# A first norm whose root is applied to the product's result too, its scales and weights loaded first; the roots of four feed-forward norms spread by a product on a repeated column

## What is computed

```
def rmsnorm(x, g):
    y = xf * lax.rsqrt(jnp.mean(xf * xf, axis=-1, keepdims=True) + RMS_EPS)
    return (y * g.astype(jnp.float32)).astype(x.dtype)
...
    for l in range(DEPTH):
        h = rmsnorm(x, norm_mix[l])
        (u_ssm, q_lat, kv_lat, k_rope, hg_q, hg_f, hg_i, hg_g, gate_logits) = jnp.split(h @ w_in[l], split_at, axis=-1)
        y_ssm = s5_mixer(u_ssm, ...)
...
        x = x + swiglu_ffn(rmsnorm(x, norm_ffn[l]), ffn_w_gate_up[l], ffn_w_down[l])
```

## Time and profile before

| | |
|---|---|
| median of 3 executions | 1955.02 us (1954.1 to 1955.06) |
| the profiled execution's own time | 1958.95 us |
| its span (first to last instruction) | 1957.1 us |
| TensorE busy | 1831.5 us, 94% |
| VectorE busy | 1163.9 us, 59% |
| ScalarE busy | 869.0 us, 44% |
| GpSimd busy | 164.0 us, 8% |
| mean DMA rate | 140 GB/s |

### The profile page before, as it was taken

How to read it: one execution, slowest core, us unless ns; L and a number is a source line. 1 busy time by engine, 2 the same in 40 slices (tenths; PEclk the granted TensorE clock), 3 DMA queues, 4 the chain that set the end, 5 groups by cost and what they waited for, 6 DMA issues and landing times.

```text
span 1957.1 us, 26609 instructions
## 1 busy us (share of the span) xinstructions
PE 1831.5 (94%) x9873; PEld 1417.2 (72%) x9873; DVE 1163.9 (59%) x1871; ACT 869.0 (44%) x1417; POOL 164.0 (8%) x203
## 2 busy tenths in 40 slices
PE   7999999989999999999888999998899999889998
PEld 6675556569898865556577998646799874669987
DVE  7993545545667893545454556565477746546775
ACT  4223434355345422334455445436455543555553
POOL 4000004020000000002112000101300000130000
PEclk9999999999999999999999999998999999899999
DMA  5444333335455444434153556431355544135553
GB/s 158 129 131 141 119 129 118 131 112 162 152 182 195 119 132 130 140 124 156 44 178 116 180 186 193 147 119 54 119 173 173 182 152 125 59 97 164 171 189 134
DMA packets 192357, 274.58 MB, mean 140 GB/s; under 512 B 25616, under 2 KB 129540, under 8 KB 192228
## 3 DMA queue, kind: packets, MB, share of 16 engines
q1 hardware_dynamic: 191364, 269.86, 44.2%
q0 software_dynamic: 864, 3.02, 0.5%
HBM read 271.78 MB, written 1.05 MB: 139 GB/s over the span
## 4 chain that ended last, share of the span: by engine, by line
PE 81%; DVE 8%; ACT 5%; issue 3%; POOL 1%; DMA 0%; SPq 0%; DVEq 0%; ACTq 0%; POOLq 0%
PE bank L390 41%; PE bank L388 30%; DVE WL L1132 2%; ACT WH L1375 2%; PE bank L649 1%; PE bank L570 1%; POOL WL L1132 1%; PE bank L992 1%; PE bank L578 1%; PE bank L842 1%; PE bank L473 1%; DVE bank L2022 1%; ACT HTH L1375 1%; PE bank L696 1%; DVE HTL L1969 1%
## 5 line engine op out<-in xcount | busy, mean ns | idle before, releaser
L1375 ACT ACTIVATE WH<-W 128x1024 fp32r<-128x1024 f32 x328 | 347.5, 1060 | 325.8 <-PE bank L390 251.8
L1132 DVE TENSOR_TENSOR WL<-W,WH 128x1024 fp32r<-128x1024 f32 x288 | 353.1, 1226 | 229.4 <-ACT WH L1375 221.1
L390 PE MATMUL bank<-HTH,WH 128*128 128x256 f32 x1536 | 440.9, 287 | 24.6 <-DVE WL L1132 14.7
L390 PE MATMUL bank<-HTL,WH 128*128 128x256 f32 x1536 | 436.5, 284 | 0.0
L390 PE MATMUL bank<-HTH,WL 128*128 128x256 f32 x1536 | 436.4, 284 | 0.0
L390 PEld LDWEIGHTS bank<-HTH,WH 128*128 128x128 f32 x1536 | 296.5, 193 | 31.3 <-DVE WL L1132 17.7
L390 PEld LDWEIGHTS bank<-HTL,WH 128*128 128x128 f32 x1536 | 296.8, 193 | 0.5 <-issue 0.5
L390 PEld LDWEIGHTS bank<-HTH,WL 128*128 128x128 f32 x1536 | 296.6, 193 | 0.0
L388 PE MATMUL bank<-W,HTF 128*128 128x512 f32 (+1 forms) x576 | 230.1, 557 | 0.0
L390 PE MATMUL bank<-WH,HTH 128*128 128x512 f32 x480 | 196.1, 409 | 15.5 <-POOL WL L1132 9.3
L390 PE MATMUL bank<-WH,HTL 128*128 128x512 f32 x480 | 191.8, 400 | 0.0
(11 more groups left out here) (400 smaller groups left out, 2208.0 us busy)
## 6 DMA issues: line engine op xcount, KB each, us to landing
W<-in_w_in SPq DMA_DIRECT2D x132, 512.0 KB, 3.6
W<-in_ffn_w_gate_up SPq DMA_DIRECT2D x176, 256.0 KB, 3.1
W<-in_w_up SPq DMA_DIRECT2D x176, 256.0 KB, 3.1
W<-in_ffn_w_down SPq DMA_DIRECT2D x44, 512.0 KB, 4.2
W<-in_w_down SPq DMA_DIRECT2D x44, 512.0 KB, 4.3
W<-in_w_out SPq DMA_DIRECT2D x32, 512.0 KB, 4.0
W<-in_ssm_w_glu SPq DMA_DIRECT2D x16, 512.0 KB, 3.6
W<-in_x_w_kv SPq DMA_DIRECT2D x16, 512.0 KB, 4.1
```

What stands on the lines that cost most here:

```text
L390: m = pe.matmul(out, at_a(a[x]), at_b(b[y]), start=(start and i == 0), stop=(stop and i == 2), skip_group_check=True)
L1132: eng.tensor_tensor(WL[:, m % HSLOTS, 0:width], W[:, n % RSLOTS, 0:width], h, ALU.subtract)\
L1375: copy = lambda dst, src, scale=1.0: act.activation(dst, src, ACT.Copy, scale=scale)
```

## The change

Four things change.

1. The first layer's first norm is treated like the second layer's: TensorE transposes `X` itself, the eviction multiplies by the scale alone (into `HTLF`), `ssm_u` runs on that, and VectorE multiplies each `u` by `RB` as it evicts it. VectorE also writes `HTF` = `HTLF` times `RB` for the products behind it (two instructions on 128x1024). VectorE's second half of `setup_states` becomes `setup_steps` and stands behind that, and the second group of phases stands between the `u`.
2. The 16 rows of `norm_mix` are loaded on their own, right behind `X`, then the first weight chunk, then the other parameters, then the other chunks. TensorE transposes the scales alone first (`par0`), and the other parameters between the first and the second `u`. GpSimd makes the identity and the index tables first, masks later.
3. `token_row` no longer needs the copy in `SCR`: the stationary operand is the column of `RSTD` itself, repeated 128 times by its access pattern. It waits for the root alone. GpSimd's copies are gone.
4. In the four feed-forward layers `token_row` stands behind the last chunk of pair 0, one chunk earlier.

```diff
             def token_row(n):
 
-                pe.wait_ge(sem["rstd_rows"], rows_at[n])
+                pe.wait_ge(sem["rstd"], n + 1)
                 ps = begin("rb", n)
                 for tt in range(TT):
-                    m = pe.matmul(ps[:, tt * P:tt * P + P], RSR[:, tt, :], IDENT[:, :], start=(tt == 0),
+                    m = pe.matmul(ps[:, tt * P:tt * P + P], RSTD[:, n, tt:tt + 1].broadcast_to([P, P]), IDENT[:, :], start=(tt == 0),
                                   stop=(tt == TT - 1), skip_group_check=True)
...
+                    pe.wait_ge(sem["x_rows"], 16)
+                    for j in range(4):
+                        raw_T(nrm, j, None)
...
-                    src = HTLF if l else HTF
+                    src = HTLF
...
-                ssm_u(0, 1)
                 if l:
-                    token_row(mix_norm)
+                    ssm_u(0, 1)
+                else:
+                    ssm_u(0)
+                    parameters()
+                    ssm_u(1)
+                token_row(mix_norm)
                 ssm_u(2)
...
-                if l:
-                    pe.wait_ge(sem["mix_scaled"], 1)
+                pe.wait_ge(sem["mix_scaled"], l + 1)
...
-                            if (j, k0) == (1, 0):
+                            if (j, k0) == (0, KT - 2):
                                 token_row(n)
...
+            sp.dma_start(R1[0:16, :], T["norm_mix"].rearrange("l (k p) -> (l k) p", p=P)).then_inc(sem["mix_rows"], 16)
...
             for n, (name, srcs, k, cols) in enumerate(chunks):
+                if n == 1:
+                    first_params()
...
-                if n in rows_at:
-                    signal(pool.tensor_copy(RSR, RSTD[:, n, :].rearrange("p (t o) -> p t o", o=1)
-                                            .broadcast_to([P, TT, P])), "rstd_rows", rows_at[n])
...
-                    norm_rows(nrm, X)
-                    norm_cols(nrm, "norm_mix", l)
+                    whole_cols(nrm, HTLF, mix_gain, 0)
+                    whole_cols(nrm, HTLF, mix_gain, 2)
+                    sum_x()
+                    parameters()
                     setup_states()
...
-                else:
-                    for q in range(4):
-                        take_u(q)
```

More of the change, by code:

```diff
@@ L465, in raw_T @@
             def raw_T(n, j, tag):
-                for tt in range(TT):
+                for tt in range(TT) if tag else ():
                     freed(*tag, tt, j // 2)
@@ L1542, in take_PT, with sum_x, parameters @@
                 evict(t_buf(tag, i).rearrange("p a b -> p (a b)"), tag, "t", m)
[L1544 to L1550, removed]
-            ps = bank(("par",))
-            copy(PAR[:, 0:NR1], ps[:, 0:NR1])
-            free_after(copy(PAR[:, C3:CLS + 32], ps[:, C3:CLS + 32]), "par")
-            signal(act.activation(SST[:, 0, :], PAR[:, CLS:CLS + 32], ACT.Exp), "sst_step", 1)
+            wait_full(act, ("par0",))
+            free_after(copy(PAR[:, 0:16], bank(("par0",))[:, 0:16]), "par0")
+            def sum_x():
+                act.wait_ge(sem["x_rows"], 16)
+                for tt in range(TT):
+                    ins = act.activation(XN[:, tt, :], X[:, tt, :], ACT.Square, scale=DM ** -0.5,
+                                         accum_out=SSQ[:, 0, tt:tt + 1])
+                    if tt < TT - 1:
+                        link(ins)
+                signal(ins, "ssq", 1)
+            def parameters():
+                act.wait_ge(sem["params"], 16 * N_PARAMS)
+                signal(copy(LSB.rearrange("p (g c) -> p g c", g=2), LSR.rearrange("p (g o) -> p g o", o=1)
+                            .broadcast_to([32, 2, 64])), "ls_rows", 1)
+                full("par")
+                ps = bank(("par",))
+                copy(PAR[:, 16:NR1], ps[:, 16:NR1])
+                free_after(copy(PAR[:, C3:CLS + 32], ps[:, C3:CLS + 32]), "par")
+                signal(act.activation(SST[:, 0, :], PAR[:, CLS:CLS + 32], ACT.Exp), "sst_step", 1)
             def tables(l, q):
@@ L2166, in setup_states, with setup_steps @@
                 signal(tt_(e[:, 1, :], lb1, d, ALU.subtract), "sst", 1)
-                for q in range(2):
-                    for _ in phases(0, q):
-                        pass
+            def setup_steps():
+                lre, lim = PAR[:, C3:C3 + 32], PAR[:, C3 + 32:C3 + 64]
                 dve.wait_ge(sem["sst_act"], 1)
@@ L2273, in _, with take_u @@
             for l in range(DEPTH):
+                def take_u(q):
+                    wait_full(dve, ("u", l, q))
+                    free_after(tt_(UT[:, q, :], bank(("u", l, q))[:, 0:S], RB, ALU.mult), "u", l, q)
+                mix_gain = lambda k: gain("norm_mix", l, k, KT)
                 if l == 0:
-                    norm_rows(nrm, X)
-                    norm_cols(nrm, "norm_mix", l)
+                    wait_freed(dve, ("par0",))
+                    for j in (1, 3):
+                        whole_cols(nrm, HTLF, mix_gain, j)
@@ L2277, in _ @@
                     setup_states()
                 else:
-                    def take_u(q):
-                        wait_full(dve, ("u", l, q))
-                        free_after(tt_(UT[:, q, :], bank(("u", l, q))[:, 0:S], RB, ALU.mult), "u", l, q)
-                    add_whole(nrm, HTLF, lambda k: gain("norm_mix", l, k, KT), ("ffd", l - 1), RSTD[:, nrm - 1, :])
-                    for _ in phases(l, 2):
-                        pass
-                    wait_freed(dve, ("rb", nrm))
-                    take_u(0)
@@ L2288, in _ @@
-                    take_u(1)
-                    for _ in phases(l, 3):
-                        pass
-                    take_u(2)
-                    for j in range(0, KT // 2, 2):
-                        wait_freed(dve, ("hT", nrm, j))
-                    for k in range(0, KT, 4):
-                        ins = tt_(HTF[:, k:k + 4, :], HTLF[:, k:k + 4, :],
-                                  RB.rearrange("p (o t) -> p o t", o=1).broadcast_to([P, 4, S]), ALU.mult)
-                    signal(ins, "mix_scaled", l)
@@ L2298, in _ @@
-                    take_u(3)
+                    add_whole(nrm, HTLF, mix_gain, ("ffd", l - 1), RSTD[:, nrm - 1, :])
+                for _ in phases(l, 2 if l else 0):
+                    pass
+                wait_freed(dve, ("rb", nrm))
+                take_u(0)
+                take_u(1)
+                for _ in phases(l, 3 if l else 1):
+                    pass
+                take_u(2)
+                for j in range(0, KT // 2, 2):
+                    wait_freed(dve, ("hT", nrm, j))
@@ L2299, in _ @@
+                for k in range(0, KT, 4):
+                    ins = tt_(HTF[:, k:k + 4, :], HTLF[:, k:k + 4, :],
+                              RB.rearrange("p (o t) -> p o t", o=1).broadcast_to([P, 4, S]), ALU.mult)
+                signal(ins, "mix_scaled", l + 1)
+                take_u(3)
+                if l == 0:
+                    setup_steps()
                 nrm += 1
```

83 lines of the change are left out of this document (44 added, 39 removed).

## The result

The changed kernel takes 1945.56 us (median of 6 executions, 1943.12 to 1946.9), the kernel before 1955.11 on the same chip (6 executions, 1954.1 to 1959.31). The ratio is 0.9943, 95% interval 0.993 to 0.9956: 11.2 us less, between 8.6 and 13.7, where 7.1 was forecast. The direction was right and the size too small. A second measurement gave 0.9941 (0.9922 to 0.9959).

What follows compares the result with a forecast made beforehand. TensorE, busy for 94% of the span, was taken as the bound. Feed-forward layers 5.8, second layer's norm 0 and start 1.3 summed to 7.1 us off 1955.02, so 1947.9 us, range 1945 to 1951.5.

Steps and rivals of the forecast that it cites:

- Feed-forward layers: TensorE's waits for `WL` at the four feed-forward starts go: 5.8 us gained, bounds 4.2 to 6.2.
- The repeated column: `token_row` with the repeated column costs the same as the load from `SCR`: 0 us, at worst 3 us lost.
- The second layer's norm: Second layer's first norm: the 0.4 us wait for GpSimd's copy ends, TensorE waits for VectorE's scaling instead; 0.0 us gained.
- The start: Kernel start, up to the long products: 1.3 us gained, taken between 2.2 and 0.5; range −1.0 to 3.2.
- Both ends of the bound: At the start, the range's ends: −1.0 if half speed lasts into the long products, 3.2 if SyncE's rows come sooner.
- SyncE's rows came 1.0 us sooner: At the start, rows were put at 29.8; a microsecond sooner, with three chunks in a row instead of four, gave 3.2.
- the pause costs more: Rival at the start: TensorE stays at half clock into `hf`, −1.0 instead of 1.3, 1950.2 us; start worth nothing or less: 0.18.
- VectorE at the start: VectorE's set-up begins at 14 and the first scan at 35.2, 2.5 us sooner, so VectorE takes nothing back.
- The stall did not move elsewhere: Rival in the four feed-forward layers: the stall moves, 0.9 us lost in each, 1951.5 us; stalls only half gone: 0.11.
- the parameters came in time: Rival at the start: parameters come late behind a 512 KB chunk and the kernel slows, 1971 us for 24 us delay; chance 0.03.
- The base: The starting time of the whole kernel, from which the forecast gain was taken: 1955.02 us, median of the runs shown.

Runs made afterwards that it cites:

- e3: The kernel before with the repeated column as the stationary operand and without GpSimd's copies, nothing moved: ratio 1.0002.
- e7: The changed kernel, with the first matrices' transposes waiting for their own four transfers alone and ScalarE evicting `BT` ahead of its second cosine: ratio 0.9925.
- e9: The changed kernel with 3.6 us of dense work at the four former stops, three products in the first two feed-forward layers, two in the others: ratio 0.9971.
- e10: The changed kernel with 13.0 us of dense work at the four former stops, ten products in the first two feed-forward layers, eight in the others: ratio 0.9996.

## Why the prediction was right or wrong

**Feed-forward layers: right mechanism, mis-sized price.** "Sum: 2 × 1.70 + 2 × 1.22 = 5.8 us": the recorded waits fell by 5.8. The step that failed is the price of a stop: I took its recorded idle time and put the clock behind it at nothing, counting the clock at the start alone. Measured, the part gives 9.6 (5.9 to 13.3). Of this 6.6 stand in the trace, since each of the four stops costs 0.1 to 0.3 us more from start to start than the idle time recorded. The other 3.0 go with the clock of these executions, 0.9837 against 0.9814, worth 3.8 us by the line. That a stop brings half clock is shown for the long ones, in 4 of 4. For the short ones it is seen behind 3 of 18, and at none of 50 places without a stop; each such stretch loses 0.43 × 4 = 1.7 us by the windows of 1079 to 1083, which makes 4 × 3/18 × 1.7 = 1.1 on average. What moved the clock beyond that stays open.

**A term that was missing.** The sum had nothing for the transfer of `out`, which lands 0.9 us sooner behind its issue. The cause stays open.

**The whole.** Forecast 7.1, measured 11.2 (8.6 to 13.7): 0.8 more at the stops, 0.7 more at the start, 0.9 at the last transfer. This leaves 1.7, inside the interval, for which the mean clock of the change (0.983 and 0.9823 against 0.9814, worth 1.5 to 2.6) is enough.

**The repeated column: right**, 0.60 us as before, and e3 at 1.0002.

**The second layer's norm: right.** The wait went to the scaling (0.6 us instead of 0.4), and nothing was gained.

**The start: right in direction, 1.3 where 2.0 came.** Both ends of the bound happened together. SyncE's rows came 1.0 us sooner, the case that I had left to the range (the reason that I gave for it, fewer chunks on its queue, was not tested), and the whole stretch ran at half clock, as feared. That the two nearly cancel is luck. The window of 35 to 36 shows the clock back before the long products, so the rival "the pause costs more" did not come.

**VectorE at the start: put 1.3 us too early.** I put the set-up at 14; ScalarE's parameter steps stand behind the sums of squares, and it began at 15.28. It took nothing back, with 0.35 us to spare; in e7 it took most of a further gain of 1.7 us.

**The other rivals.** The stall did not move elsewhere (no new wait for `WL`), and the parameters came in time.

**The base.** The median of three that was shown, 1955.02, is 1.7 under the median of 88 executions; this touches the forecast in us, not the ratio.

## What to carry to other kernels

Price a wait of TensorE from start to start of the matmuls around it, not by the idle time recorded; look at the granted clock in the window behind it, and expect single executions of the same kernel to differ by the clock's share. Compare the last transfer too, for it is on the path. A new bound is rarely alone: compare when the other engine's result is ready with when it is read, for the spare time there is all that a further gain can keep. Sort a surplus of a few us by groups of kernels, since one run beside one run could not tell three theories apart here, and set each group's mean clock beside it before the surplus is put down to the clock.

## What was not expected of the hardware

- One unchanged kernel, on one core of each of four chips, ranged over 15 us (1945.21 to 1960.75), and its mean granted clock over 0.979 to 0.987; 0.001 of clock went with 1.65 us.
- Stops of 4.1 to 4.6 us were followed by half clock in 4 of 4 cases, stops of 1.2 to 1.7 us in 3 of 18, and no half clock stood at 50 places where the stop was gone.
- Two kernels without any of the four stops, which differ only in how much dense work they add (e9 and e10), ran at mean clocks of 0.9801 and 0.9831.
- The same transfer of 1 MB at the end of the kernel took 4.0 us from its issue in 13 kernels and 4.9 in five; the new start is what sets them apart.
- A column of a tile repeated 128 times as the stationary operand costs what a stored copy costs: 0.60 us for `token_row` either way.
